# Summing the conditioning's row blocks on VectorE instead of TensorE, in a kernel of two transformer blocks

## What is computed

```python
sc, scc = silu(c), silu(c_ctx)                  # (1, 1024), (1024,)
mod_x = sc @ w_ada[0] + b_ada[0]                # w_ada: 1024 x 6144
mod_c = scc @ w_ada[0] + b_ada[0]
sh1, sc1, g1, sh2, sc2, g2 = split(mod_x, 6)
csh1, csc1, *_ = split(mod_c, 6)                # of the context only shift 1 and scale 1 are used
ux = (rms_norm(x, norm1) * (1 + sc1) + sh1) @ w_in
uc = (rms_norm(xc, norm1) * (1 + csc1) + csh1) @ w_in
... attention, Fourier and convolution heads on ux, uc
x = x + g1 * mix_out(...)
h = rms_norm(x, norm2) * (1 + sc2) + sh2        # routed experts on h, result times g2
```

## Time and profile before

| what | us |
|---|---|
| median of 3 runs | 1936.45 |
| lowest, highest | 1935.86, 1939.63 |
| the profiled execution | 1936.95 |
| its span in the profile | 1935.1 |
| PE busy | 1843.1 (95%) |
| DVE busy | 883.8 (46%) |
| ACT busy | 730.4 (38%) |

### The profile page before, as it was taken

One profiled execution on the slowest core, in us unless ns is written; L12 is line 12 of the kernel. 1 busy time (PEld: TensorE's weight loads), 2 busy tenths in 40 slices (PEclk: granted clock), 3 DMA queues, 4 the chain that ended last, 5 costly groups with the idle time before them and its releaser, 6 DMA issues.

```text
span 1935.1 us, 29860 instructions
## 1 busy us (share of the span) xinstructions
PE 1843.1 (95%) x11586; PEld 1423.9 (74%) x11586; DVE 883.8 (46%) x1274; ACT 730.4 (38%) x1168; POOL 107.6 (6%) x112
## 2 busy tenths in 40 slices
PE   5999899999999979999999999999999998899998
PEld 2876544434444359998899996899989997759998
DVE  4243322222122154455877773545555544635454
ACT  3353222212112144434555552444444443634433
POOL 1010000000000000001212210000000001200000
PEclk8999899999999989999999999999999998999999
DMA  9865499999999965666754542566466655026653
GB/s 375 302 239 202 164 415 420 421 422 422 422 423 422 421 203 174 195 177 165 218 150 116 149 108 65 148 179 194 130 197 194 181 172 208 1 72 189 193 177 107
DMA packets 317322, 441.92 MB, mean 228 GB/s; under 512 B 11846, under 2 KB 270406, under 8 KB 289350
## 3 DMA queue, kind: packets, MB, share of 16 engines
q1 hardware_dynamic: 314424, 431.59, 64.5%
q0 software_dynamic: 2560, 8.40, 1.3%
q10 hardware_dynamic: 272, 1.05, 0.2%
HBM read 439.95 MB, written 1.05 MB: 228 GB/s over the span
## 4 chain that ended last, share of the span: by engine, by line
PE 78%; DMA 13%; DVE 4%; ACT 2%; POOL 1%; issue 1%; SPq 0%; POOLq 0%; DVEq 0%; ACTq 0%
PE PS L255 26%; PE PS L265 12%; DMA R<-w_up 10%; PE PS L349 10%; PE PS L1930 6%; PE PS L1541 4%; PE PS L1991 3%; PE PS L1904 2%; PE PS L636 1%; PE PS L1673 1%; PE PS L1042 1%; PE PS L421 1%; DMA R<-w_ada 1%; DMA R<-w_down 1%; PE PS L495 1%
## 5 line engine op out<-in xcount | busy, mean ns | idle before, releaser
L255 PE MATMUL PS<-XH,HI 128*128 128x256 f32 x1408 | 401.8, 285 | 1.1 <-DVE XL L129 1.0
L255 PE MATMUL PS<-XL,HI 128*128 128x256 f32 x1408 | 400.6, 285 | 0.0
L255 PE MATMUL PS<-XH,LO 128*128 128x256 f32 x1408 | 400.4, 284 | 0.0
L255 PEld LDWEIGHTS PS<-XH,HI 128*128 128x128 f32 x1408 | 272.0, 193 | 6.5 <-issue 2.5
L255 PEld LDWEIGHTS PS<-XL,HI 128*128 128x128 f32 x1408 | 272.0, 193 | 3.8
L255 PEld LDWEIGHTS PS<-XH,LO 128*128 128x128 f32 x1408 | 272.0, 193 | 0.0
L189 DVE TENSOR_TENSOR LO<-RAW,HI 128x2048 fp32r<-128x2048 f32 x84 | 192.6, 2293 | 117.2 <-ACT HI L178 117.2
L198 ACT ACTIVATE HI<-RAW 128x1024 fp32r<-128x1024 f32 x88 | 93.8, 1065 | 293.6 <-PE PS L265 293.6
L222 DVE TENSOR_TENSOR LO<-RAW,HI 128x1024 fp32r<-128x1024 f32 x88 | 107.8, 1225 | 195.0 <-ACT HI L198 195.0
L1930 PE MATMUL PS<-SPLIT,ARENA 128*64 128x512 f32 x512 | 169.7, 594 | 10.9 <-DMA R<-w_up 10.9
L178 ACT ACTIVATE HI<-RAW 128x2048 fp32r<-128x2048 f32 x88 | 167.9, 1908 | 3.8 <-DMA RAW<-ffn_w_in 2.3
(11 more groups left out here) (341 smaller groups left out, 2936.9 us busy)
## 6 DMA issues: line engine op xcount, KB each, us to landing
RAW<-ffn_w_in SPq DMA_DIRECT2D x176, 512.0 KB, 5.1
R<-w_down SPq DMA_DIRECT2D x64, 1024.0 KB, 17.4
SPLIT<-w_up SPq DMA_DIRECT2D x48, 1024.0 KB, 22.8
RAW<-w_gate SPq DMA_DIRECT2D x46, 1024.0 KB, 20.0
RAW<-ffn_w_out SPq DMA_DIRECT2D x88, 512.0 KB, 3.5
RAW<-a_w_in SPq DMA_DIRECT2D x69, 512.0 KB, 5.2
R<-w_ada SPq DMA_DIRECT2D x24, 1024.0 KB, 7.6
SPLIT<-w_gate SPq DMA_DIRECT2D x16, 1024.0 KB, 22.0
```

The lines of the kernel that those rows point to most:

```text
L255: m = e.matmul(GU[j][:, T * q:T * q + T], gu(w, j)[:, q, k, :], x[:, k, :], start=(k == 0 and n == 0), stop=(k == KT - 1 and n == 2))
```

## The change

Group 0 stays with PE, but the stationary operand has 32 columns instead of 2: `M.CS` is now 32 wide, cleared by POOL, the two vectors in its first two columns. So the sums fill all 128 partitions of the bank (mostly zeros), and `rows_out` is one copy of 128 partitions instead of four of two.

For groups 1 and 2, which need the latent side alone, DVE computes on each of the 128 partitions the weighted sum over the eight blocks, 2048 columns at once (`weighted_rows`): a tensor_scalar for the group's first block, a scalar_tensor_tensor (block times its conditioning column, plus the sum so far) for the other seven, 16 instructions in all. The sum `M.ACC` takes 2048 columns of SBUF. PE puts the bias into PSUM (`bias_row`, four matmuls) and adds up the 128 partitions of `M.ACC` with a stationary operand of ones (`partition_sums`, four matmuls). Between the two groups, DVE's first block of group 2 waits for group 1's partition sums.

Places: `bias_row(1)` behind use 1, `partition_sums(1)` behind use 6, `turn_rows(1)` behind use 7, `bias_row(2)` behind use 8, `partition_sums(2)` in step 1, `turn_rows(2)` in step 3; on ACT `rows_out(1)` behind use 6's copy and `rows_out(2)` at the start of step 2. On DVE: three blocks before chunk 2's low part, then 2, 3, 4, 1 and 1 blocks behind the low parts of chunks 2 to 6, and one in each of steps 0 and 1 behind the masking; the copy of group 2's columns in step 3. The scores of the attention move from the slot 1 of R to columns of the high/low buffers that the context side used; some buffers change places.

```diff
+    def weighted_rows(n):
+        g, m = divmod(n, 9)
+        slot, u = n % R_SLOTS, n // R_SLOTS
+        v.wait_ge(s.r_in[slot], 16 * u + 16)
+        w, c = M.R[:, SR * slot:SR * slot + SR], M.CS[:, m - 1, 0:1]
+        if m == 1:
+            v.wait_ge(s.cs, g)
+            x = v.tensor_scalar(M.ACC, w, c, None, ALU.mult)
+        else:
+            v.wait_ge(s.r_used[(n - 1) % R_SLOTS], (n - 1) // R_SLOTS + 1)
+            x = v.scalar_tensor_tensor(M.ACC, w, c, M.ACC, ALU.mult, ALU.add)
+        x.then_inc(s.r_used[slot], 1)
+
+    def bias_row(g):
+        first = 9 * g
+        at_least(e, s.mr, 4 * g)
+        e.wait_ge(s.r_in[first % R_SLOTS], 16 * (first // R_SLOTS) + 16)
+        bias = M.R[0:1, SR * (first % R_SLOTS):SR * (first % R_SLOTS) + SR]
+        for q in range(4):
+            mm = e.matmul(AB[32 * q:32 * q + 32, :], M.ONES[0:1, 0:32], bias[:, 512 * q:512 * q + 512], start=True, stop=False)
+        mm.then_inc(s.r_used[first % R_SLOTS], 1)
+
+    def partition_sums(g):
+        last = 9 * g + 8
+        e.wait_ge(s.r_used[last % R_SLOTS], last // R_SLOTS + 1)
+        for q in range(4):
+            mm = e.matmul(AB[32 * q:32 * q + 32, :], M.ONES[:, 0:32], M.ACC[:, 512 * q:512 * q + 512], start=False, stop=True)
+        mm.then_inc(s.cs, 1)
...
-        for q in range(4):
-            a.activation(M.MR[32 * q:32 * q + 2, g, :], AB[32 * q:32 * q + 2, :], ACT.Copy).then_inc(s.mr, 1)
+        a.activation(M.MR[:, g, :], AB, ACT.Copy).then_inc(s.mr, 4)
...
-    PRODUCTS = [2, 2, 2, 2, 1, 0, 2, 2, 2, 3]
...
-    SC = lambda n, h: M.R[:, SR + 1024 * (n % 2) + 512 * h:SR + 1024 * (n % 2) + 512 * h + 512]
+    SC = lambda n, h: M.SPLIT[:, (8192, 11264)[n % 2] + 512 * h:(8192, 11264)[n % 2] + 512 * h + 512]
...
-        for c in range(2, 8):
+        rows = [n for n in range(10, 27) if n % 9]
+        sum_rows(3)
+        for c, count in ((2, 2), (3, 3), (4, 4), (5, 1), (6, 1), (7, 0)):
             low(c)
+            sum_rows(count)
             if c == 5:
                 columns_out(1)
```

More of the change, by code:

```diff
@@ L1169, in product @@
             e.wait_ge(s.cs, 1)
-            e.wait_ge(M.ones_set, 3)
+            e.wait_ge(M.ones_set, 4)
         e.wait_ge(s.r_in[slot], 16 * u + 16)
@@ L1175, in product @@
             rhs = M.R[:, SR * slot + 512 * q:SR * slot + 512 * q + 512]
-            lhsT = M.ONES[0:1, 0:2] if m == 0 else M.CS[:, m - 1, :]
-            mm = e.matmul(AB[32 * q:32 * q + 2, :], lhsT, rhs[0:1] if m == 0 else rhs, start=m == 0, stop=m == 8)
+            lhsT = M.ONES[0:1, 0:32] if m == 0 else M.CS[:, m - 1, :]
+            mm = e.matmul(AB[32 * q:32 * q + 32, :], lhsT, rhs[0:1] if m == 0 else rhs, start=m == 0, stop=m == 8)
         mm.then_inc(s.r_used[slot], 1)
+    def weighted_rows(n):
[24 more added lines that the diff above has]
+        mm.then_inc(s.cs, 1)
     def rows_out(g):
         a.wait_ge(M.ones_set, 3)
-        a.wait_ge(s.r_used[(9 * g + 8) % R_SLOTS], (9 * g + 8) // R_SLOTS + 1)
-        for q in range(4):
-            a.activation(M.MR[32 * q:32 * q + 2, g, :], AB[32 * q:32 * q + 2, :], ACT.Copy).then_inc(s.mr, 1)
+        if g:
+            a.wait_ge(s.cs, g + 1)
+        else:
+            a.wait_ge(s.r_used[8 % R_SLOTS], 8 // R_SLOTS + 1)
+        a.activation(M.MR[:, g, :], AB, ACT.Copy).then_inc(s.mr, 4)
     def turn(g):
@@ L1196, in columns_out @@
                       MTB.rearrange("p (b q r) -> p q b r", b=4, q=4)[:, :, :, 0:2]).then_inc(s.mc, 1)
-    return load, product, rows_out, turn, columns_out
+    return load, product, weighted_rows, bias_row, partition_sums, rows_out, turn, columns_out
 def first_mixer(nc, M, A, rope_act, rope_dve):
@@ L1206, in first_mixer @@
     FB = [PS[:, 4, :], PS[:, 5, :]]
-    load, product, rows_out, turn_rows, columns_out = conditioning(nc, M, A["w_ada"], A["b_ada"])
+    load, product, weighted_rows, bias_row, partition_sums, rows_out, turn_rows, columns_out = conditioning(nc, M, A["w_ada"], A["b_ada"])
     w_in_v = A["w_in"].rearrange("(k p) n -> p k n", p=128)
@@ L1224, in first_mixer @@
     LAST_USE = {c: n for n, c, *_ in USES}
-    PRODUCTS = [2, 2, 2, 2, 1, 0, 2, 2, 2, 3]
-    N_FIRST = len(PRODUCTS)
+    N_FIRST = 10
     STEPS = 8
     SCORES, OB = [PS[:, 2, :], PS[:, 3, :]], PS[:, 0, 0:T]
-    SC = lambda n, h: M.R[:, SR + 1024 * (n % 2) + 512 * h:SR + 1024 * (n % 2) + 512 * h + 512]
+    SC = lambda n, h: M.SPLIT[:, (8192, 11264)[n % 2] + 512 * h:(8192, 11264)[n % 2] + 512 * h + 512]
     PT = lambda h: (M.m_PT, M.MR[:, 0])[h]
@@ L1303, in act @@
         a.wait_ge(s.c_in, 16)
-        a.activation(M.CS[:], M.CRAW[:], ACT.Silu).then_inc(M.ada.cs, 1)
+        a.wait_ge(M.ones_set, 4)
+        a.activation(M.CS[:, :, 0:2], M.CRAW[:], ACT.Silu).then_inc(M.ada.cs, 1)
         def square(n):
@@ L1366, in act @@
             use_out(n)
-            if n == 4:
+            if n == 6:
                 rows_out(1)
-        rows_out(2)
         for k in range(STEPS + 2):
+            if k == 2:
+                rows_out(2)
             if k % 2 == 0 and k >= 2:
@@ L1443, in divided, with sum_rows @@
                 v.tensor_scalar(SC(n, h), SC(n, h), stat(M.RC, n, h), None, ALU.mult).then_inc(t_.p_ready, 1)
-        for c in range(2, 8):
+        rows = [n for n in range(10, 27) if n % 9]
+        def sum_rows(count):
+            for _ in range(count):
+                weighted_rows(rows.pop(0))
+        sum_rows(3)
+        for c, count in ((2, 2), (3, 3), (4, 4), (5, 1), (6, 1), (7, 0)):
             low(c)
+            sum_rows(count)
             if c == 5:
@@ L1452, in dve @@
                 shifted(k)
+            if k < 2:
+                sum_rows(1)
             if k >= 1:
                 divided(k - 1)
-            if k == 1:
+            if k == 3:
                 columns_out(2)
@@ L1638, in pe @@
                 use_half(n, m)
-            for _ in range(PRODUCTS[n]):
-                product(ada)
-                ada += 1
+            if n == 1:
+                bias_row(1)
             if n == 6:
+                partition_sums(1)
+            if n == 7:
                 turn_rows(1)
+            if n == 8:
+                bias_row(2)
         for k in range(STEPS + 2):
@@ L1649, in pe @@
                 use_half(N_FIRST + k // 2, k % 2)
-            if k == 0:
+            if k == 1:
+                partition_sums(2)
+            if k == 3:
                 turn_rows(2)
@@ L2203, in program @@
         M.GC = sb("GC", [128, N_GC])
-        M.XH, M.XL = sb("XH", [128, KT, T], f32r), sb("XL", [128, KT, T], f32r)
+        M.XH = sb("XH", [128, KT, T], f32r)
+        with nc.sbuf_tensor("SPARE", [128, 3072], f32) as M.SPARE:
+            pass
+        M.XL, M.HH, M.HL = sb("XL", [128, KT, T], f32r), sb("HH", [128, 2, T], f32r), sb("HL", [128, 2, T], f32r)
         M.RAW = sb("RAW", [128, 2, SLOT])
@@ L2242, in program @@
         M.WF = carve(2, FH, at=11268)
-        M.MC, M.CRAW, M.CS = carve(96), carve(KT, 2), carve(KT, 2)
+        M.MC, M.CRAW = carve(96), carve(KT, 2)
+        M.CS = M.SPARE[:, 2048:2048 + 32 * KT].rearrange("p (k n) -> p k n", k=KT)
         M.MSC, M.SH2, M.ONES = carve(3, KT), carve(KT), carve(128)
@@ L2259, in program @@
         M.mix_OT = carve(KT, T, at=7168)
+        M.ACC = carve(SR, at=7168)
         M.FA, M.m_PT, M.CHP = carve(2, 512, at=9216), carve(512), carve(2, T + 2)
@@ L2434, in _ @@
             p.memset(M.MR, 0.0).then_inc(M.ones_set, 1)
-            p.wait_ge(M.ones_set, 3)
+            p.memset(M.CS, 0.0).then_inc(M.ones_set, 1)
+            p.wait_ge(M.ones_set, 4)
             mixer[2]()
```

2 lines of the change are left out of this document (removed).

## The result

The changed kernel took 1927.31 us, the median of 5 runs (1925.49 to 1931.6), against 1936.45 us (1935.77 to 1939.63) for the kernel before: a ratio of 0.995, with a 95% interval of 0.9935 to 0.9964. It is 9.1 us faster where 5.3 us were forecast; the forecast time was 1931.2 us, and the range of 1926 to 1936 us holds the result. That is a right answer with two wrong terms in it, as the rest shows: the mixer gave less than was forecast (2.6 us by the two profiles, 4.3 us by the times of run e2), and a part of the change that had been costed at nothing gave a gain of the same size.

What follows compares the result with a forecast made beforehand. PE was taken to bound the mixer, then DVE's queue behind block 23's load: PE's step 2 comes 5.73 us earlier, 5.3 us after 0.44 us of turning, so 1936.45 - 5.3 = 1931.2 us; range 1926 to 1936 us.

Steps and rivals of the forecast that it cites:

- Early stage: Group 0's rows out of PSUM: one copy for four starts chunk 0's high part and PE 0.63 us earlier.
- 3.5 us of low clock: PE behind its early idle: clock at 0.50 until some 3.5 us beyond the first matmul of that stretch.
- PE in the middle: PE from the transposes to group 2's bias: 18 products removed, four quads added; 51.82 us, ending at 97.52 us.
- rival (4): PE's products: four of 32 columns no longer run side by side; 9 us slower, 1945 us; chance 0.03.
- The load of block 23: DVE's wait: the load's slot frees only behind group 2's bias; landing takes 6.6 us (bounds 5.3 and 10.1), at 104.15 us.
- DVE's queue: DVE from block 23's landing to the first division's end: 17.23 us, to 121.38 us, 5.73 us earlier than before.
- rival (3): DVE's rows: scalar_tensor_tensor at half rate, 4.58 us each; step 2 11.7 us later, 1948.6 us; chance 0.07.
- The turning of group 2's rows: PE in step 2 onward: this 0.44 us now lies on PE's path, leaving 5.3 us of the gain.
- From step 2 to the end: Experts' weight stream and all after it: the mixer's gain is kept to the end; w_down issued at 202 to 203 us.
- Moving the scores ... and the high and low buffers past each other ...: nothing: SBUF layout: moving these buffers changes no instruction's size and the experts' first slots stay clear, so it costs nothing.
- (1): End of the mixer: block 23's load lands in time, chunk 7 bounds; step 2 at 116.4 us, 1926.1 us; chance 0.06.
- (2): Same mechanism, dearer: later landing, 3.03 us rows or low clock before chunk 6; 1933 to 1937.5 us; chance 0.22.

Runs made afterwards that it cites:

- e2: The changed kernel with HH and HL behind STATS again and all other buffers at their old places: 1934.27 us, ratio 0.9978 to the kernel before.
- e3: The changed kernel with group 2's bias product behind use 7 instead of use 8: 1929.35 us, ratio 0.9946 to the kernel before; again 1928.09 us, 0.9935.
- e4: The kernel before with only the 32-column products (all 27) and one copy out of PSUM per group: 1937.95 us, ratio 0.9994.
- e9: e3 with SP holding back the loads of blocks 25 and 26 until chunk 7 of w_in has landed: 1918.95 us, ratio 0.9893 to the kernel before.
- e7: e3 with group 1's bias product also moved, ahead of use 0: 1924.87 us, ratio 0.9926 to the kernel before; again 1925.86 us, 0.9934.
- e1: The kernel before with only HH and HL moved directly behind XL, as in the changed kernel: 1931.17 us, ratio 0.9966.
- e5: The kernel before with only HH and HL moved directly behind HI and LO: ratio 0.9966.
- e8: The kernel before with only HH and HL moved just ahead of the small buffers, 468 words lower: ratio 0.9965.

## Why the prediction was right, and where it was wrong

**Early stage: right.** Chunk 0's high part was put at 30.58 us and stood at 30.64, and PE reached the first use 0.57 us earlier (41.82 against 42.39). The use then ran longer at the lower clock (4.81 us against 3.94), so the transposes came at 46.62 us, 0.92 us later than the sum had them. That is no cost of the change: the sum had started from the kernel before's trace, in which the clock rose early, and with the same code this use took up to 5.74 us in other traces. The end of the use stands at a mean of 46.7 us in the seven traces with the new early part (both of the changed kernel, e2, both of e3, e4, e9: 45.87 to 47.41; e7 has one more product there and is left out) and of 47.3 us in the five with the code of before (46.33 to 48.11), 0.6 us apart as forecast. The prediction counted 3.5 us of low clock from "the first matmul of that stretch"; that holds from the first use's start at 37.02 us, while four transposes had already run from 31.24 us.

**PE in the middle: right.** From the transposes to the end of group 2's bias the sum had 51.82 us, and the trace has 98.26 - 46.62 = 51.64 us. (Two small slips in sums: 97.52 + 6.6 + 0.05 is 104.17 and not 104.15 us, and rival (4)'s five times 2.91 us is 14.6 and not 14.2 us. Neither changes a conclusion.) Partition sum and bias product took 0.99 to 1.06 us each, against 0.97.

**The load of block 23: right in mechanism, a term mis-sized.** It was the wait on DVE, as forecast. From issue to landing 6.6 us were taken, with bounds of 5.3 and 10.1; it was 8.4 us here, 7.9 us when the kernel was run again and 8.1 us in e2. This is the term of the sum that was too small. In the kernel before, SP issued the four loads behind that row one by one between 92.9 and 102.1 us; here they went out together, from 98.3 to 99.6 us, with chunk 7's at 97.31, so that each got a smaller share of the rate (the last one landed after 14.5 us); that the bunching is the reason is argued from this and from e9's shorter landing. The bias's 0.74 us (it ended at 98.26 us, forecast 97.52, by the late clock) and the load's 1.8 us are the whole difference between step 2 at 121.38 and at 123.90 us, and so w_down went out at 205.25 us and not at 202 to 203. The bounds held.

**DVE's queue: right.** 17.23 us were forecast from the landing to the end of the first division. The last instruction of that division is

```profile
123.49 0.48 DVE L1475 TENSOR_SCALAR SPLIT<-SPLIT,STATS 128x512 f32<-128x512 f32 x1
```

and 123.97 - 106.70 = 17.27 us. PE went from the row to step 2 by way of the partition sum (1.06 us), which the sum had not set beside the division; the two end within 0.1 us of each other, so it cost nothing here. The row took 2.350 us, forecast 2.35, so rival (3) is refuted for 128x2048 too. The Trainium skill (Vector Engine (DVE) Microarchitecture Reference, section 7, "Points that are easy to get wrong") says that two non-bf16 sources in SBUF halve the throughput, and doesn't say against what. Read as half the rate of a tensor_tensor, as the prediction did, it doesn't hold here: that takes 2.285 us. Against the tensor_scalar of the same size, which reads one tensor, the trace comes near it, 2350 ns against 1284, 1.83 times:

```profile
L1187 DVE TENSOR_SCALAR ARENA<-R,SPARE 128x2048 f32<-128x2048 f32 x2 | 2.6, 1284 | 2.1 <-PE PS L1206 2.1
```

The turning of group 2's rows and what follows it cost 0.59 us on PE's path (from step 2 to w_down's issue 81.35 us against 80.76), forecast 0.44.

**From step 2 to the end: right.** What was gained at step 2, less that, arrived at w_down's issue: 3.21 - 0.59 = 2.62 us. Both are figures of one pair of traces. The five traces with the conditioning code of before have step 2 at 128.0 us on average, the three with the whole change (twice the changed kernel, and e2) at 124.0 us (123.90 to 124.20): 4.0 us, of the 5.73 forecast, and 3.5 us at w_down, of 5.3. That fits e2's 4.3 us (2.3 to 6.4).

**"Moving the scores ... and the high and low buffers past each other ...: nothing": wrong.** This is the step that failed outright. The operands' places changed while their sizes didn't, and the argument looked at sizes only. The runs show a matmul of L265 faster by 0.047 us / 12 = 3.9 ns, which makes 4.1 us, and a time shorter by 6.6 us in e1 (4.3 to 8.9). By the mechanism that was forecast, the kernel of e2 (1934.27 us) is the one that was predicted, and it gained 4.3 us of the 5.3 forecast. The 1927 us of the changed kernel lie in the range, but by way of a part that was not in the sum: that the total came out right is in part luck.

**The rivals.** (1) did not happen in the changed kernel, because the slot rule holds. Its sum, 116.4 us for step 2 and 10.3 us in all at w_down, is about what e9's trace reached once the load was out of the way: 116.21 us, and 207.87 - 197.55 = 10.3 us. That they agree to 0.2 us is partly luck: the clock rose early in e9's trace (transposes at 45.87 us, where the sum has 45.70). (2) in its dear-landing part is half of what happened; its clock did fall behind the idle before chunk 6 (0.55 from 108.5 to 112 us) and was hidden behind DVE's queue, as that text said. (4) is refuted by e4.

**What stays open.** Beyond the pace, e1, e5 and e8 were 2.5 us faster than their 4.1 us explain. From the first L265 to the end of the span 1213.8 to 1215.1 us passed with the old place and 1206.9 to 1210.5 us in eight of the ten traces with the new one, but 1213.7 us in the first trace of e3 and 1213.2 us in the first of e7, which have it too. Traces of one kernel differ there by up to 5.1 us, and the granted clock accounts for it: e3's two traces have 34.1 and 27.3 us at half clock in this stretch, a loss of 3.4 us for 3.2 us of time, e7's have 39.9 and 29.6 us, 5.2 us for 5.1. With half of the low stretches taken off, the four traces with the old place stand at 1198.0 to 1200.4 us and the ten with the new one at 1192.9 to 1196.8 us; the means are 4.0 us apart, which is the pace and nothing more. A line through the timed executions of the kernel before gives 1.0 us less time for each 0.001 more of mean granted clock (29 executions beside e1, 18 beside e5; 0.6 us in the last 11). The executions of e1 and e8 had a mean clock of 0.9812 and 0.9814, the kernel before beside them 0.9793 and 0.9795: an estimate of 1.9 us of their 2.5. e5 had 0.9798 against 0.9795, which explains nothing. Whether the layout has a hand in the clock is not shown. Nor is what sets the moment at which the clock rises in the mixer.

## What to carry to other kernels

A buffer that is moved to make room is an edit of its own: time it alone, and look at the pace of the largest group of matmuls that read it. When a load is made late by a slot that is held longer, list what else will be asked for in the same microseconds; moving the late load earlier handed most of the wait to the next one (e3: 2.4 us gained at step 2 where 6.5 were expected), and holding back, on top of that, the loads that nobody needs yet gave more than sending the needed one sooner (e9, 1918.95 us against 1928.09 us of e3 in the same group). The length of a burst behind an idle PE depends on when the clock rises, and that scattered from 39.8 to 46.7 us in the fourteen traces here; a difference of a microsecond there between two traces says nothing about the change until other traces of the same code have been put beside them.

## What the hardware showed that was not expected

- The pace of a matmul with 128x128 fp32 weights and 512 moving columns depends on where the weights lie in SBUF: 8.547 or 8.500 us per period with 12 of them, to the hundredth of a microsecond the same in every one of the fourteen traces with the one place or the other.
- Chunk 7's load of 1 MB, asked for by POOL, landed after 7.3 us behind two of SP's loads and after 11.2 us behind four: the transfers of both engines share one rate. In the second case the queues together moved 387 GB/s from 98 to 109 us, with the transfers busy all the time.
- The same code, started at the same time, can find the clock high or low. Behind the same idle stretch the 30 matmuls of the first use took 3.94 us from 42.39 us on in one trace and 5.74 us from 42.38 us on in another.
- A scalar_tensor_tensor of 128x2048 with two fp32 sources in SBUF takes 2.350 us, 3% more than a tensor_tensor of that size (2.285 us); a tensor_scalar of that size, with one tensor to read, takes 1.284 us.
